# Two load buffers instead of four, and small moves in the delta rule, in a two-block transformer kernel on one core

## The reference

```
mod = silu(c) @ w_ada + b_ada            # 1024 -> 6 * 1024
shift1, scale1, gate1, shift2, scale2, gate2 = split(mod, 6)
h    = rmsnorm(x, g1) * (1 + scale1) + shift1
proj = h @ w_in                          # sliding-window, differential attention, gates
x    = x + gate1 * (merged @ w_out)
h2   = rmsnorm(x, g2) * (1 + scale2) + shift2
x    = x + gate2 * conv_ffn(h2)
return rmsnorm(x, final_g)
```

## Time and profile before

| what | value |
|---|---|
| median of three executions | 1254.33 us |
| time of the profiled execution | 1255.49 us |
| its span in the profile | 1253.6 us |
| PE busy | 1161.3 us (93%) |
| DVE busy | 611.2 us (49%) |
| ACT busy | 497.8 us (40%) |
| POOL busy | 495.4 us (40%) |
| loads of pieces | 96 of 256 KB, 2.9 us to landing in the median |
| loads of weight blocks of the first `w_in` and second `w_in` | 66 of 512 KB, 5.7 us |

### The profile page before, as it was taken

One profiled execution on the slowest core, in us unless ns is written; L12 is line 12 of the kernel. 1 busy time (PEld: TensorE's weight loads), 2 busy tenths in 40 slices (PEclk: granted clock), 3 DMA queues, 4 the chain that ended last, 5 costly groups with the idle time before them and its releaser, 6 DMA issues.

```text
span 1253.6 us, 15604 instructions
## 1 busy us (share of the span) xinstructions
PE 1161.3 (93%) x5616; PEld 918.0 (73%) x5616; DVE 611.2 (49%) x1195; ACT 497.8 (40%) x810; POOL 495.4 (40%) x387
## 2 busy tenths in 40 slices
PE   6997999997798797999999997997999999989997
PEld 5776777774697575777777775875888888878886
DVE  3276877547674326256665675525534343320003
ACT  5346444364342325444433456424433333311124
POOL 4443233344322333423331332553345555434443
PEclk9998999988799898999999998998999999999999
DMA  8575565410130032244432221233233333321311
GB/s 173 130 157 128 125 129 135 135 42 1 42 94 1 13 118 84 76 135 135 137 125 68 68 68 34 101 117 100 70 100 91 86 91 100 100 101 67 100 67 67
DMA packets 114286, 116.32 MB, mean 93 GB/s; under 512 B 4817, under 2 KB 97191, under 8 KB 114228
## 3 DMA queue, kind: packets, MB, share of 16 engines
q1 hardware_dynamic: 98800, 86.58, 25.7%
q10 hardware_dynamic: 14212, 26.13, 6.6%
q0 software_dynamic: 1216, 2.83, 0.7%
HBM read 113.41 MB, written 2.12 MB: 92 GB/s over the span
## 4 chain that ended last, share of the span: by engine, by line
PE 65%; issue 14%; POOL 10%; DVE 6%; ACT 4%; DMA 1%; POOLq 0%; ACTq 0%; SPq 0%; DVEq 0%
PE bank L642 16%; PE bank L643 15%; PE bank L644 15%; POOL wlo L448 10%; PE bank L792 3%; PE bank L817 2%; PE bank L800 2%; PE bank L913 2%; PE bank L924 2%; PE bank L721 1%; PE bank L702 1%; PE bank L677 1%; PE bank L937 1%; ACT whi L1158 1%; DVE att_qk L1625 0%
## 5 line engine op out<-in xcount | busy, mean ns | idle before, releaser
L448 POOL TENSOR_TENSOR wlo<-raw,whi 128x512 fp32r<-128x512 f32 x312 | 421.3, 1381 | 610.1 <-ACT whi L1158 610.1
L642 PE MATMUL bank<-h_hi,whi 128*128 128x512 f32 x1016 | 417.8, 411 | 26.3 <-DVE h_lo L1497 18.0
L643 PE MATMUL bank<-h_lo,whi 128*128 128x512 f32 x1016 | 401.5, 395 | 0.0
L644 PE MATMUL bank<-h_hi,wlo 128*128 128x512 f32 x1016 | 400.6, 394 | 0.0
L642 PEld LDWEIGHTS bank<-h_hi,whi 128*128 128x128 f32 x1016 | 194.5, 191 | 91.5 <-issue 37.7
L644 PEld LDWEIGHTS bank<-h_hi,wlo 128*128 128x128 f32 x1016 | 194.0, 191 | 42.4
L643 PEld LDWEIGHTS bank<-h_lo,whi 128*128 128x128 f32 x1016 | 194.6, 192 | 40.6 <-issue 3.4
L1158 ACT ACTIVATE whi<-raw 128x2048 fp32r<-128x2048 f32 (+1 forms) x79 | 150.3, 1902 | 175.4 <-PE bank L644 165.6
L1279 ACT ACTIVATE pT_a<-bank 128x256 f32<-128x256 f32 (+3 forms) x80 | 32.4, 405 | 198.2 <-PE bank L800 198.2
L642 PE MATMUL bank<-ffn_hi,whi 128*128 (+1 forms) x176 | 70.0, 398 | 4.1 <-DVE ffn_lo L1497 4.1
L1594 DVE SCALAR_TENSOR_TENSOR ada_acc<-ada_w,small,ada_acc 128x512 f32<-128x512 f32 x84 | 71.4, 850 | 0.0
(11 more groups left out here) (310 smaller groups left out, 1491.0 us busy)
## 6 DMA issues: line engine op xcount, KB each, us to landing
raw<-w_in SPq DMA_DIRECT2D x66, 512.0 KB, 5.7
ada_w<-w_ada ACTq DMA_DIRECT2D x96, 256.0 KB, 2.9
raw<-w_up SPq DMA_DIRECT2D x44, 512.0 KB, 4.6
raw<-w_down SPq DMA_DIRECT2D x22, 512.0 KB, 4.0
raw<-w_out SPq DMA_DIRECT2D x16, 512.0 KB, 4.6
x_tok<-x SPq DMA_DIRECT2D x4, 512.0 KB, 5.4
toe<-bias_rows POOLq DMA_DIRECT2D x8, 256.0 KB, 7.1
raw<-w_branch_swa SPq DMA_DIRECT2D x4, 512.0 KB, 3.5
```

Source lines behind the costliest of these rows:

```text
L448: ins = pool.tensor_tensor(wlo[s][:, c], raw[s][:, c], whi[s][:, c].bitcast(F32), ALU.subtract)
L642: pe.matmul(ps, wh, h_hi, start=start, stop=False)
L643: pe.matmul(ps, wh, h_lo, start=False, stop=False)
L644: return pe.matmul(ps, wl, h_hi, start=False, stop=stop)
```

## The change

1. `ada_w` has two buffers instead of four. Piece p may be loaded when piece p - 2 is used. In the attentions ACT's load stands at the end of a unit, behind the copy of that unit's probabilities (and the split of a weight block, where there is one), and is for the next unit.
2. The pieces are used earlier: 16 in S0 (one after each of the tiles 1 to 8, two after each of the tiles 9 to 12), then 32 in `a1`, 8 in the solve, 8 in S1, 32 in `a2`, none in S4. `fold(0)` stands between the two tiles of block 5 and `fold(1)` behind the transposes of v, ahead of the first projection steps outside of S0.
3. In the preparation, the product for the decays goes to bank 5 and behind the last norm sum and the waits for tiles 29 to 32; DVE's copy and ACT's `egc` follow it. `vb` is made by ACT in four 128 x 128 steps a chunk instead of by DVE in one.
4. The squares of the delta rule's q and k have buffers of their own, and POOL makes the low part of block 17 (`lo(N_S1)`) ahead of the preparation instead of behind it.

```diff
...
         top[0] = toe_at
-        nry4, nryy4 = ([sb(f"dn_{k}{s}", [P, SEQ]) for s in range(4)] for k in ("ry", "ryy"))
+        nsq4, nry4, nryy4 = ([sb(f"dn_{k}{s}", [P, SEQ]) for s in range(4)] for k in ("sq", "ry", "ryy"))
         ends.append(top[0])
-        nsq4 = [at(f"dn_sq{s}", [P, SEQ], offset=V + 4096 + 2048 * s)[0] for s in range(4)]
...
         ends.append(top[0])
-        dn_end = top[0]
...
         assert top[0] <= nc.sbuf_usable_end
-        ada_w += [at(f"ada_w{s}", [P, SEQ], offset=dn_end + 2048 * (s - 2))[0] for s in (2, 3)]
...
-        ADA_S0 = {T: (T - 5, T - 4) for T in range(5, 13)}
-        ADA_A1, ADA_DN, ADA_S1, ADA_A2, ADA_S4, ADA_N = 8, 40, 48, 56, 88, 96
+        ADA_S0 = {T: (T - 1, T) if T <= 8 else (2 * T - 10, 2 * T - 8) for T in range(1, 13)}
+        ADA_A1, ADA_DN, ADA_S1, ADA_A2, ADA_N = 16, 48, 56, 64, 96
...
                 pool.tensor_tensor(nsq4[j % 4][:, :], qkv[:, k, :], qkv[:, k, :], ALU.mult).then_inc(S["sq_done"], 1)
+            lo(N_S1)
...
             start_xt(pool, TT - 1)
-            lo(N_S1)
...
                     pe.wait_ge(S["rms_lo"], before("n0", "lo") + 1)
-                gemm(n, tiles_of(n)[0], (0,) if n == 0 else (0, 1), ready=(S["rms_lo"], before("n0", "lo") + 1) if n == 0 else None)
+                if n == 5:
+                    gemm(n, tiles_of(n)[0], (0,))
+                    fold(0)
+                    gemm(n, tiles_of(n)[1], (1,))
+                else:
+                    gemm(n, tiles_of(n)[0], (0,) if n == 0 else (0, 1), ready=(S["rms_lo"], before("n0", "lo") + 1) if n == 0 else None)
...
             mm.then_inc(S["v_tr"], 1)
+            fold(1)
             gate_steps(dil_steps, -1)
-            fold(0)
...
                 gate_steps(norm_steps, w)
-                if w == 0:
-                    pe.wait_ge(S["g_ready"], 1)
-                    pe.wait_ge(S["in_masks"], 16)
-                    pe.wait_ge(S["att_out"], 4)
-                    pe.matmul(bank[6][:, 0:16], m(C_TRIU), gdec, start=True, stop=True).then_inc(S["dn_gct"], 1)
+            pe.wait_ge(S["g_ready"], 1)
+            pe.wait_ge(S["in_masks"], 16)
+            for T in range(29, 33):
+                evac(pe, T)
+            pe.wait_ge(S["nt_done"], 16)
+            pe.matmul(bank[5][:, 0:16], m(C_TRIU), gdec, start=True, stop=True).then_inc(S["dn_gct"], 1)
                 pe.wait_ge(S["dn_gtri"], 2 * c + 2)
-                if c < 2:
-                    evac(pe, 32 - c)
-                    pe.wait_ge(S["nt_done"], 13 + c)
...
                     pe.wait_ge(S["norm_done"], 16)
-                    pe.wait_ge(S["mod_add"], ADA_DN // 8)
+                    pe.wait_ge(S["mod_add"], 6)
...
                 if c == 0:
-                    pe.wait_ge(S["mod_add"], ADA_S1 // 8)
+                    pe.wait_ge(S["mod_add"], 7)
...
             pe.wait_ge(S["v2_ready"], 5)
-            pe.wait_ge(S["mod_add"], ADA_S4 // 8)
+            pe.wait_ge(S["mod_add"], 12)
...
             norm_sum("n2", 2, 7)
-            fold(ADA_S4 // 8)
...
                     f, kt = divmod(p, KT)
-                    if p >= 4:
-                        act.wait_ge(S["ada_piece"], p - 3)
-                    act.dma_start(ada_w[p % 4][:, :], a["w_ada_2"][0, kt * P:(kt + 1) * P, f * SEQ:(f + 1) * SEQ])\
-                        .then_inc(S[f"ada_in{p % 4}"], 16)
+                    if p >= 2:
+                        act.wait_ge(S["ada_piece"], p - 1)
+                    act.dma_start(ada_w[p % 2][:, :], a["w_ada_2"][0, kt * P:(kt + 1) * P, f * SEQ:(f + 1) * SEQ])\
+                        .then_inc(S[f"ada_in{p % 2}"], 16)
...
             act.activation(csil, colA[:, ROWS_A["c"]:ROWS_A["c"] + 8], ACT.Silu).then_inc(S["csil_ready"], 1)
+            ada_loads(2)
...
                         hi(n + 2)
-                    if T == 3:
-                        ada_loads(3)
-                    elif T in ADA_S0:
-                        ada_loads(ADA_S0[T][1] + 2)
+                    if T >= 1:
+                        ada_loads(ADA_S0[T][1] + 1)
...
                     exps(w + 1)
-                    if tag != "a3" and w < len(units):
-                        ada_loads((ADA_A1 if tag == "a1" else ADA_A2) + w + 3)
...
                     tail(w)
+                    if tag != "a3" and w < len(units):
+                        ada_loads((ADA_A1 if tag == "a1" else ADA_A2) + w + 2)
...
             ln_exp()
-            act.wait_ge(S["dn_egc"], 1)
-            act.activation(egc, gc, ACT.Exp).then_inc(S["dn_egc"], 1)
...
+            act.preload_act_table_set("natural_log_exp_and_others")
+            act.wait_ge(S["dn_egc"], 1)
+            link(act.activation(egc, gc, ACT.Exp))
...
                 ins.then_inc(S["dn_kv"], 1)
+                act.wait_ge(S["dn_ktr"], 2 * c + 2)
+                for h in range(DN_H):
+                    ins = act.activation(vb[:, c, h, :], bank[7][:, h * P:(h + 1) * P], ACT.Copy,
+                                         scale=beta[:, 4 * c + h:4 * c + h + 1])
+                ins.then_inc(S["dn_kv"], 1)
+            for T in range(29, 33):
+                evac(act, T)
                     if c % 2 == 1 and l < 4:
-                        ada_loads(ADA_DN + 2 * l + c // 2 + 3)
+                        ada_loads(ADA_DN + 2 * l + c // 2 + 2)
...
                     squares("n1", kt, xT[:, kt, :], nsq)
-                    ada_loads(ADA_S1 + kt + 3)
+                    ada_loads(ADA_S1 + kt + 2)
...
                     squares("n2", kt, xT[:, kt, :], nsq)
-                    ada_loads(ADA_S4 + kt + 3)
...
                     dve.wait_ge(S["csil_ready"], 1)
-                dve.wait_ge(S[f"ada_in{p % 4}"], 16 * (p // 4 + 1))
+                dve.wait_ge(S[f"ada_in{p % 2}"], 16 * (p // 2 + 1))
                     mod_add(f)
-                    ins = dve.tensor_scalar(ada_acc[:, :], ada_w[p % 4][:, :], csil[:, 0:1], None, ALU.mult)
+                    ins = dve.tensor_scalar(ada_acc[:, :], ada_w[p % 2][:, :], csil[:, 0:1], None, ALU.mult)
                     dve.wait_ge(S["ada_piece"], p)
-                    ins = dve.scalar_tensor_tensor(ada_acc[:, :], ada_w[p % 4][:, :], csil[:, kt:kt + 1], ada_acc[:, :],
+                    ins = dve.scalar_tensor_tensor(ada_acc[:, :], ada_w[p % 2][:, :], csil[:, kt:kt + 1], ada_acc[:, :],
...
                         small_vectors()
-                    if T in ADA_S0:
-                        ada()
+                    if T >= 1:
+                        for _ in range(*ADA_S0[T]):
+                            ada()
...
-            mod_add(ADA_DN // 8)
+            mod_add(6)
             scale_col(g1c, ROWS_A["norm1_g"], 8)
-            dve.wait_ge(S["dn_gct"], 1)
-            dve.tensor_copy(gc, bank[6][:, 0:16]).then_inc(S["dn_egc"], 1)
...
             dve.wait_ge(S["tile_ready"], 33)
+            dve.wait_ge(S["dn_gct"], 1)
+            dve.tensor_copy(gc, bank[5][:, 0:16]).then_inc(S["dn_egc"], 1)
+            dve.wait_ge(S["dn_egc"], 1)
...
                 dve.tensor_tensor(attnT[:, c], four(bank[2 + c % 2][:, :]), Dk[c % 2][:, :, :], ALU.mult).then_inc(S["dn_dtb"], 1)
-                dve.wait_ge(S["dn_ktr"], 2 * c + 2)
-                dve.tensor_tensor(vb[:, c], four(bank[7][:, :]), over(beta[:, four_c]), ALU.mult).then_inc(S["dn_kv"], 1)
...
             attention("a2", units_a2(), lambda h: dve.wait_ge(S["in_alibi"], 16), tail2)
-            mod_add(ADA_S4 // 8)
+            mod_add(ADA_N // 8)
...
                                              op0=ALU.mult, op1=ALU.add).then_inc(S[f"evac{T % 4}"], 1)
-                    ada()
             norm_h2("n2", g2c)
-            mod_add(ADA_N // 8)
```

## The result

The changed kernel takes 1315.29 us (median of 4 runs, 1312.68 to 1316.37) against 1254.91 us beside it, a ratio of 1.0472 with a 95% interval of 1.0445 to 1.05. The direction was forecast, the size was not: 1277 was forecast, with 1264 to 1291 as the range.

A forecast was written before the change was run, and what follows sets the result against it. TensorE, busy 93% of the span, was taken as the bound, so delays count only where it waits. Terms 6.5 + 7.6 + 8 + 1 + 0 + 0 = 23 us on 1255.5 gave 1278.6, 1277 against the median; range 1264 to 1291.

The forecast's parts named there:

- its three places: Late piece loads make PE wait in the first projection (6.5 us), the delta-rule solve (7.6) and the first attention (8).
- First attention, 8 us: First attention: most units hide the late load; waits near weight blocks, units 18, 30 and the last fold sum to 8 us.
- the clock as a risk: First attention: a gap in PE can lower its clock as at 100 us; given as a reason for the wide bounds.
- rival (b): Both attentions: loads become their clock, 16 us in the first, 5 in the second, 2 for clock; 1292 us, chance 0.15.
- the long landing: First attention: a load beside a weight block takes 9.6 us, costing PE 3.4 us, then 2 us more at the next.
- the page's sum: DMA landing time: fixed 2.0 us plus bytes over 436 GB/s, an estimate of 2.6 us for a 256 KB piece.
- First projection, 6.5 us: End of first projection: ACT waits for DVE's pieces, delaying rsqrts, v transposes and fold; 6.5 us, bounds 3 and 10.
- Solve, 7.6 us: Delta-rule solve: four waits of 1.4 us for loads issued one piece ahead, plus 2 us; 7.6 us, bounds 3 and 11.
- the 2 us for a block in the way: Delta-rule solve: 2 us added because one of seven loads, issued beside a weight block, took longer.
- Preparation, 0 us: Delta-rule preparation: vb off DVE gains 1.8 us, late decays and ACT copies lose 1.8; net nothing, bounds -2.4 and +3.
- Second attention, 1 us: Second attention: PE has 3 to 6 us to spare, only the last piece and fold cost; 1 us, bounds 0 and 6.
- the FFN, 0: Stage before the FFN: eight pieces and a fold disappear inside PE's wait for the norm; nothing gained, at most 1 us.

The follow-up runs named there:

- the light blocks: Changed kernel, but weight blocks 9 to 16, arriving during the first attention, load only a quarter of their bytes: 1281.14 us, ratio 1.0197.
- One turn earlier: Changed kernel, but each adaLN load in both attentions issued right behind the unit's exponentials, ahead of the probabilities' copy; still two buffers: 1279.55 us, ratio 1.0198.
- the block behind the load: Changed kernel, but SyncE holds weight blocks 11 to 18 until ScalarE's copy, so the adaLN load goes ahead of the block: 1290.88 us, ratio 1.0292.

## Why the prediction was wrong, step by step

*What bounds the kernel, the starvation of the pieces, its three places, its direction:* right. DVE waits for its own loads 56 times, and PE behind it exactly at the three places named.

*First attention, 8 us, bounds 1 and 18; measured 40.6.* This step failed. It said that the block in flight matters at one unit, half at another. I had read which loads met a block in the trace of before and kept that pattern, though the change moves the loads against the blocks: the one that went out up to 0.8 us ahead of each block goes out 0.6 to 1.8 us behind it, at all six. The experiments give the pieces of the sum: 9.2 us for a lead of one without long landings, 31.4 us for the blocks' bytes. In another cut, by engine, it is 27.8 us of gaps and 12.8 us of lower clock behind them. I had named the clock as a risk and given it nothing. The prediction also stopped each delay at PE's slack, though the late turn delays the next issue; that loop was rival (b), with 1292 us and a chance of 0.15. Its sign, an attention more than 15 us longer, came, but not as it was meant: it gave 16 us to quiet landings, which cost 9.2 with the light blocks. One turn earlier, with landings as long as before, 34 us are back, which fits the loop; but it is lead too, and no run parts the two. Block order, block bytes and lead are not additive either: each of the three alone takes away 23 to 34 of the 40.6 us, as if a stop needed all of them. One count would have come near: six blocks, times the 5.4 us that I had given to the long landing, is 32 us.

*The rule on the queues.* The Trainium skill, DMA: Bandwidth & Descriptors, section Queues, rings and completion order, says that each DMA engine takes packets in turn from the queues that have work. By that rule a 256 KB load on ScalarE's queue would share with SyncE's block and not wait for it; doubling the variable part of the page's sum (section Anatomy of one DMA, a fit to DMAs issued by GpSimd) gives an estimate of 3.2 us. The trace does not agree: 8.1 us when issued 0.96 us behind the block, 2.8 us when 0.46 us ahead of it. Two things differ. No packet of the piece moved for 4.3 us (the load issued at 198.00 ahead of the block began to move within 1 us), and meanwhile the block moved at 185 GB/s, less than half of the sum's 436. Behind those 4.3 us both queues' packets do mix, as the rule says; where the piece waited until then, no view shows.

*First projection, 6.5 us, bounds 3 and 10; measured 12.3.* The mechanism was right and the term was mis-sized. I took 5.5 us for the landing of one load; a load behind the block of 93.16 took 13.6, and later ones also came late to DVE, by up to 1.85 us. And 2.9 us of the delay lay ahead of the place from which I counted: piece 9's load went out at 103.27 and not at 100.36. The fold and the transposes ran at the lower clock (3.65 and not 1.94 us). The folds, costed at nothing but for the last, made PE wait 0.7 us in all.

*Solve, 7.6 us; measured 4.4.* Right, in the bounds. The landings were 2.7 us and not 2.9, and the 2 us for a block in the way did not come.

*Preparation, 0 us; measured 1.0.* The start lost 2.7 us (I had 1.8). The chunks gained 1.7 as forecast, but vb was mis-sized (0.5, not 1.8); the late decays gave the rest. A right sum from two wrong terms.

*Second attention, 1 us; measured 0.6, and the FFN, 0; measured -0.1.* Right. The second attention is loaded in the same way, and DVE waits there for its loads too, 31.9 us in 20 waits. But at seven of its eight blocks the nearest load goes out 0.4 us behind or 0.5 us ahead of the block (2.1 us behind at the first), the halves of its blocks land in 3.8 to 5.9 us, no piece takes more than 4.2 us, and PE waits for none but the last fold (0.5 us). No run separates these.

## What to carry to other kernels

Before a load is moved or its lead shortened, write down every other transfer beside the new issue time, not the old one: its landing may be that of the large transfer in front of it. Count how often such a transfer comes by, and take the sum as that many delays. What protects is the time from issue to use, counted in units of the loop, and not the number of buffers. And where a gap of some us opens in front of TensorE, count the lower clock behind it as a term of its own: here it was nearly half of the gaps once more. That holds for gaps of this length: with the block behind the load, where none of the eight waits for probabilities is longer than 4.2 us, PE idled 13.5 us more than before and was busy 3.7 us more (clock 0.98).

## What the runs showed of the hardware that I had not expected

- Two DMA issues 1 us apart on two engines' queues: the small one behind took 8.1 us, and 2.8 us when it went 0.46 us ahead. A load of 64 KB beside or behind a block still took 3.9 us or more.
- A single gap of 9.2 us in PE: granted clock 1.00 to 0.50, and back at 0.96 in 200 to 204 us, 4 us after PE's work resumed at 196.4.
- Blocks of the same 1 MB differ. In the changed kernel the two halves of the block issued at 177.58 landed in 8.4 and 13.9 us, those of the other five of the attention in 5.4 to 11.0. The second of the six blocks is the slowest in every kernel here, the one before too (10.9 to 11.4 us in the mean of its halves, 3.9 with a quarter of its bytes); in the changed kernel the DMA engines were 0.8 busy meanwhile, at 92 GB/s. Why was not tested.
